# Two transformer blocks on one core: new order and form of the first loads, of one norm, of the weight splits and of two feed-forwards

## The reference

```
layer 0: h += diff_attention(rms(h)); h += (silu(n @ Wg) * (n @ Wu)) @ Wd, n = rms(h)
         h += sigmoid(rms(h) @ Wgate) * (p @ Wp)
layer 1: the same, with neighbourhood attention;  h = rms(h) * norm_final
layer 2: h += even_mixer(rms(h));  h += conv_ffn(rms(h))
layer 3: h += odd_mixer(rms(h));   h += conv_ffn(rms(h));  out = rms(h) * final_norm
rms(x) = x / sqrt(mean(x * x) + 1e-6) * gamma
conv_ffn(n): u, g = n @ W_in;  a = 3-tap causal convolution of u + bias
             return (silu(a) * g) @ W_out                      (hidden width 2816)
```

## Time and profile before

| what | value |
|---|---|
| median of 3 runs | 1296.54 us (1296.34 to 1297.35) |
| the profiled execution, its own time | 1298.22 us |
| its span, first to last instruction | 1296.4 us |
| TensorE busy | 1260.0 us, 97% of the span |
| VectorE busy | 943.4 us, 73% |
| ScalarE busy | 675.2 us, 52% |
| GpSimd busy | 170.3 us, 13% |
| granted TensorE clock, mean | 0.994 of full speed |

### The profile page before, as it was taken

One profiled execution on the slowest core, in us unless ns is written; L12 is line 12 of the kernel. 1 busy time (PEld: TensorE's weight loads), 2 busy tenths in 40 slices (PEclk: granted clock), 3 DMA queues, 4 the chain that ended last, 5 costly groups with the idle time before them and its releaser, 6 DMA issues.

```text
span 1296.4 us, 22210 instructions
## 1 busy us (share of the span) xinstructions
PE 1260.0 (97%) x8648; PEld 1149.5 (89%) x8648; DVE 943.4 (73%) x1208; ACT 675.2 (52%) x971; POOL 170.3 (13%) x168
## 2 busy tenths in 40 slices
PE   6999899999999999999999899999999999999998
PEld 5899788888978888888899899999888889999986
DVE  4798787795777778777557878787757766877743
ACT  5466555544546665555446335555445566554532
POOL 4011211081120010000013702000312001000000
PEclk8999999999999999999999999999999999999999
DMA  7434598756544337775553566975464524766541
GB/s 266 159 128 128 136 246 216 209 170 206 185 150 159 130 99 207 190 194 178 179 197 130 165 207 168 263 197 178 159 203 150 163 100 129 212 185 174 192 163 64
DMA packets 277574, 224.74 MB, mean 173 GB/s; under 512 B 8424, under 2 KB 264432, under 8 KB 277376
## 3 DMA queue, kind: packets, MB, share of 16 engines
q1 hardware_dynamic: 274896, 214.24, 54.6%
q0 software_dynamic: 2608, 9.52, 2.5%
HBM read 222.67 MB, written 2.63 MB: 174 GB/s over the span
## 4 chain that ended last, share of the span: by engine, by line
PE 84%; DVE 9%; ACT 2%; DMA 2%; issue 1%; POOL 1%; SPq 1%; POOLq 0%; ACTq 0%
PE ps L1599 19%; PE ps L1590 13%; PE ps L1591 12%; PE ps L1592 12%; PE ps L1600 10%; DVE wlo L1018 3%; DVE x L1044 3%; PE ps L1598 2%; PE ps L1838 2%; ACT whi L674 2%; PE ps L1803 1%; PE ps L1805 1%; PE ps L1804 1%; PE ps L1862 1%; PE ps L1723 1%; PE ps L1891 1%
## 5 line engine op out<-in xcount | busy, mean ns | idle before, releaser
L1018 DVE TENSOR_TENSOR wlo<-raw,whi 128x2048 fp32r<-128x2048 f32 (+1 forms) x205 | 467.9, 2286 | 134.9 <-ACT whi L674 134.0
L674 ACT CAST whi<-raw 128x2048 fp32r<-128x2048 f32 (+1 forms) x205 | 384.4, 1880 | 232.7 <-PE ps L1592 136.8
L1590 PE MATMUL ps<-x,whi 128*128 128x256 f32 (+1 forms) x1640 | 474.7, 289 | 11.2 <-DVE wlo L1018 5.4
L1591 PE MATMUL ps<-x,whi 128*128 128x256 f32 (+1 forms) x1640 | 464.0, 283 | 0.0
L1592 PE MATMUL ps<-x,wlo 128*128 128x256 f32 (+1 forms) x1640 | 463.9, 283 | 0.0
L1590 PEld LDWEIGHTS ps<-x,whi 128*128 128x128 f32 (+1 forms) x1640 | 313.8, 191 | 21.3 <-issue 9.3
L1591 PEld LDWEIGHTS ps<-x,whi 128*128 128x128 f32 (+1 forms) x1640 | 314.1, 192 | 0.5
L1592 PEld LDWEIGHTS ps<-x,wlo 128*128 128x128 f32 (+1 forms) x1640 | 313.8, 191 | 0.0
L1599 PE MATMUL ps<-x,whi 128*128 128x512 f32 x616 | 222.2, 399 | 2.6 <-DVE wlo L1018 2.6
L1599 PE MATMUL ps<-hid,whi 128*128 128x512 f32 x504 | 177.7, 395 | 1.1 <-DVE hid L1312 1.1
L1600 PE MATMUL ps<-x,wlo 128*128 128x256 f32 x616 | 172.8, 280 | 0.0
(11 more groups left out here) (193 smaller groups left out, 1443.0 us busy)
## 6 DMA issues: line engine op xcount, KB each, us to landing
raw<-in_ffn_w_in SPq DMA_DIRECT2D x88, 512.0 KB, 5.1
raw<-in_ffn_w_gate SPq DMA_DIRECT2D x44, 512.0 KB, 4.0
raw<-in_ffn_w_up SPq DMA_DIRECT2D x44, 512.0 KB, 5.3
raw<-in_ffn_w_out SPq DMA_DIRECT2D x38, 512.0 KB, 4.4
raw<-in_ffn_w_down SPq DMA_DIRECT2D x32, 512.0 KB, 4.4
raw<-in_da_w_qkv SPq DMA_DIRECT2D x24, 512.0 KB, 4.9
raw<-in_na_w_qkv SPq DMA_DIRECT2D x24, 512.0 KB, 4.5
raw<-in_od_w_in SPq DMA_DIRECT2D x24, 512.0 KB, 4.6
```

The costliest lines, as they stand in the source:

```text
L674: nc.scalar.copy(whi[:, c % RING, 0:n], raw[:, c % RING, 0:n]).then_inc(w_hi, 1)
L1018: nc.vector.tensor_tensor(wlo[:, c % RING, 0:n], raw[:, c % RING, 0:n], whi[:, c % RING, 0:n].bitcast(F32), ALU.subtract).then_inc(w_lo, 1)
L1590: mm(dst, hi, x[:, 0, :], start=start, stop=False)
L1591: mm(dst, hi, x[:, 1, :], start=False, stop=False)
```

## The change

Seven edits, listed by their place in time.

1. Start. The gammas and the first x tiles are issued by ScalarE; SP begins with chunk 0 in four pieces of 256 KB, chunk 1 comes in two. The splits of chunks 0 and 1 follow the pieces, and TensorE takes chunk 0 in the order of the pieces. All four squares of the first norm stand ahead of the split of chunk 2. GpSimd makes `gmid` first and issues the constants only when chunk 2 has landed; its additions for the first norm stand behind these issues.
2. `SUM_AT` and `SPREAD_AT` of v0 and v1 move later by half a chunk or less.
3. The double norm: only the plain squares are made (four ScalarE instructions; L724 goes), GpSimd adds nothing, and TensorE forms both sums with 16 small products of the squares by `gsq` (ones and the squared gamma), two columns each.
4. The first product of layer 2 ("ev") gets banks 0, 2, 3, 5 in a written order with `EV_FREE`, and the spread moves from the middle of chunk 2 to the start of chunk 3.
5. `updates`: the low part of one weight chunk is made before the last `lo_x` and not behind it.
6. `ffn2` and `ffn3` use `wide_chunk`; for them ScalarE copies a half bank, VectorE adds and scales.
7. The masks start three chunks later in `down0` and `down2`.

```
-SUM_AT = {"v0": (2, 0), "v1": (2, 0), "v3": (1, 1)}
-SPREAD_AT = {"v0": (3, 0), "v1": (2, 1), "v3": (2, 1)}
+SUM_AT = {"v0": (2, 1), "v1": (2, 1), "v3": (1, 1)}
+SPREAD_AT = {"v0": (3, 1), "v1": (3, 0), "v3": (2, 1)}
-EV_BANKS = (2, 3, 5)
+EV_BANKS = (2, 3, 5, 0, 2, 3, 5, 2)
+EV_FREE = (0, 0, 0, 0, 1, 2, 3, 5)
-FFN_BANKS = (((5, 6), (0, 1), (2, 3)), ((5, 6), (0, 1), (2, 3)), (2, 3, 5), (5, 6, 7))
-DOWN_BANKS = ((0, 2, 5, 0), (0, 2, 5, 0), (0, 6, 0, 6))
+FFN_BANKS = (((5, 6), (0, 1), (2, 3)), ((5, 6), (0, 1), (2, 3)), ((2, 3), (0, 1), (5, 6)),
+             ((5, 6), (0, 1), (2, 3)))
+DOWN_BANKS = ((0, 2, 5, 0), (0, 2, 5, 0), (0, 5, 2, 6))
...
 SP:
-            load_x(0)
-            load_chunk("v0", 0)
+            for a in range(4):
+                cs = slice((a % 2) * 512, (a % 2 + 1) * 512)
+                sp.dma_start(dst[a // 2][:, :, cs], src[a // 2][:, :, cs]).then_inc(w0_in[a], 16)
             load_x(1)
...
 GpSimd:
-            gp.wait_ge(w0_in[1], 16)
+            nc.gpsimd.tensor_tensor(gmid[:], fin, gcol[:, GAM["mix2"]:GAM["mix2"] + KT], ALU.mult)
+            nc.gpsimd.memset(gsq[:, :, 0], 1.0)
+            nc.gpsimd.tensor_tensor(gsq[:, :, 1], fin, fin, ALU.mult).then_inc(gmid_ok, 1)
+            gp.wait_ge(w_in[2], 32)
             gp.dma_start(cst[:], consts[:, 0:NCONST]).then_inc(const_in, 16)
...
-                    gp.wait_ge(w_used, START["down0"])
+                    gp.wait_ge(w_used, START["down0"] + 3)
...
-            gp.wait_ge(w_used, START["down2"])
+            gp.wait_ge(w_used, START["down2"] + 3)
...
 ScalarE:
+            nc.scalar.dma_start(gcol[:], w["gammas"]).then_inc(gcol_in, 16)
+            nc.scalar.dma_start(h[:, 0:2, :], x_source(0)).then_inc(x0_in[0], 16)
...
+            for p in range(4):
+                squares("mix0", p)
             split(2)
-            squares("mix0", 2)
-            squares("mix0", 3)
...
 squares():
+                nc.scalar.activation(to, hpair(p), ACT.Square, scale=D ** -0.5
+                                     ).then_inc(sq_ok, 1)
...
 ScalarE, ffn, conv:
+                        ac.wait_ge(w_used, c0 + 1 + j)
+                        nc.scalar.copy(gu[:, jj, :, :], ps[:, b0:b0 + 2, S:2 * S]
+                                       ).then_inc(part_ok, 1)
                         split(c0 + jj + RING, turn)
...
 VectorE, updates:
+                    if p == 3:
+                        split(last(wname) - 1 + RING)
                     lo_x(name, p)
-                split(last(wname) - 1 + RING)
                 split(last(wname) + RING)
...
 VectorE, ffn, conv:
-                        ve.wait_ge(w_used, c0 + 1 + j)
-                        nc.vector.tensor_tensor(g, b, over2(rst[:]), ALU.mult).then_inc(gu_ok, 1)
+                        ve.wait_ge(part_ok, n)
+                        nc.vector.tensor_tensor(g, ps[:, b0:b0 + 2, 0:S], g, ALU.add
+                                                ).then_inc(sum_ok, 1)
+                        ve.wait_ge(sum_ok, n)
+                        nc.vector.tensor_tensor(g, g, over2(rst[:]), ALU.mult).then_inc(gu_ok, 1)
                         if one:
                             taps(*one)
...
 TensorE, sum_squares:
+                if n == MID:
+                    for k in range(KT):
+                        pe.wait_ge(sq_ok, sq_base(n) + k // 2 + 1)
+                        src = ssum[:, k // 2, :] if k < 4 else sq[:, k // 2 - 2, :]
+                        for t in range(TT):
+                            at = (k % 2) * S + t * P
+                            ins = mm(bank(SS)[:, 2 * t:2 * t + 2], src[:, at:at + P], gsq[:, k, :],
+                                     start=k == 0 and t == 0, stop=k == KT - 1 and t == TT - 1)
...
 TensorE, ffn:
-                    if layer < 2:
-                        wide_chunk(b, c0 + jj, xs[XBUF[name]], KT, name if fresh else None,
-                                   turn, middle=middle)
-                    else:
-                        f_chunk(b, c0 + jj, name, fresh, turn, middle)
+                    wide_chunk(b, c0 + jj, xs[XBUF[name]], KT, name if fresh else None,
+                               turn, middle=middle)
...
 TensorE, ev:
+                if EV_FREE[i]:
+                    pe.wait_ge(copied, COPY_BASE["ev"] + EV_FREE[i])
+                if i == 3:
+                    spread_r("mix2")
+                f_chunk(EV_BANKS[i], START["ev"] + i, "mix2")
```

More of the change, by code:

```diff
@@ L508, in add_squares @@
                 n = NORM[name]
-                per = sums_of(n)
+                total = ssum[:, 0, :]
                 for p in range(1, 4):
[L511 to L521, removed]
-                            gp.wait_ge(add_ok, r)
[L523 to L532, removed]
@@ L707, in squares @@
                 n = NORM[name]
[L708 to L714, removed]
-                    else:
[L716 to L726, removed]
+                r = add_base(n) + p - 1
+                if p == 0 and n:
+                    ac.wait_ge(ss_out, n)
+                if p and n != MID and r >= 2:
+                    ac.wait_ge(add_ok, r - 1)
+                if n == MID:
+                    to = ssum[:, p, :] if p < 2 else sq[:, p - 2, :]
+                else:
+                    to = sq[:, r % 2, :] if p else ssum[:, 0, :]
+                nc.scalar.activation(to, hpair(p), ACT.Square, scale=D ** -0.5
+                                     ).then_inc(sq_ok, 1)
             def pair(name, p):
@@ L912, in _ @@
             take_x("mix0", 0)
-            split_first(0)
-            split_first(1)
+            for q in range(4):
+                split_first(q)
             take_x("mix0", 1)
-            split(1)
+            split_first(4)
+            split_first(5)
             take_x("mix0", 2)
             take_x("mix0", 3)
-            squares("mix0", 0)
-            squares("mix0", 1)
+            for p in range(4):
+                squares("mix0", p)
             split(2)
-            squares("mix0", 2)
-            squares("mix0", 3)
             ac.wait_ge(lam_sum, 2)
@@ L1061, in diagonals @@
                 ve.wait_ge(pow_ok, n + 1)
-                for s in range(sums_of(n)):
+                for s in range(spreads_of(n)):
                     r = tiny[:, 12:14] if s else tiny[:, 6:8]
@@ L1780, in down @@
                         pe.wait_ge(hid_lo, base + 8 * part + D_TILES[part])
-                    if part == 0 and layer < 2 and g < 3:
+                    if part == 0 and g < 3:
                         pe.wait_ge(sum_ok, base + FT - 2 + g)
@@ L2021, in _ @@
             ffn(3)
+            pe.wait_ge(sum_ok, 4 * FT - 1)
             for k in range(KT):
```

149 lines of the change are left out of this document (90 added, 59 removed).

## The result

The changed kernel takes 1299.67 us, the median of 14 runs from 1295.92 to 1302.91. The kernel before, on the same chip, takes 1296.66, the median of 14 runs from 1294.66 to 1297.6. The ratio is 1.0021, with a 95% interval of 1.0011 to 1.003: slower by 0.2%, some 2.7 us, where 4.3 us less was forecast. It lies outside the range, and none of the rivals describes it (D names a time near it, 1299.2, but for a reason that the traces exclude).

What follows compares the result with a forecast made beforehand. TensorE, busy 97% of the span, was taken as the bound, so time could come only from its waits and streaming rate. Terms -5.3 -4.6 +3.3 -4.4 +2.6 +3.2 +2.0 -1.1 gave -4.3: 1292.2 us, range 1285.5 to 1298.5.

Steps and rivals of the forecast that it cites:

- D: Rival: VectorE becomes the bound of the convolution feed-forwards; +2.7 us, 1299.2, at 5.8 us a chunk; chance 0.14.
- part 5: Updates: later x in each first chunk costs +2.6 us of work, and clock falls behind longer waits cost +3.2.
- part 2: Start: earlier squares and sums bring v0's spread to 30 us against 34.99; -4.6 us, bounds -2.5 and -6.5.
- Part 4: Double norm, gates of layer 1 and "ev": faster low parts without GpSimd's additions, earlier pooled product; -4.4 us.
- Part 3: v1: moving the sums later adds a wait for diagonals and delays the gate; +3.3 us, bounds +1.0 and +4.5.
- Part 1: Convolution feed-forwards of layers 2 and 3: 512-column form saves 0.12 us in each of 44 chunks; -5.3 us.
- E: Rival: the 512-column form saves only 2.5 ns per tile product, 3.5 us less; -0.8 us, 1295.7; chance 0.03.
- Part 6: Loads in layer 2: a chunk's load is issued later and TensorE arrives earlier, so it waits; +2.0 us.
- Part 7: Masks and down product: masks moved later remove layer 2's wait for hidden values; -1.1 us.
- Rival B: The clock never falls and the new order in `updates` is free; -10.1 us, 1286.4; chance 0.18.
- C: Rival: GpSimd's constants delay the first sums, start gains only 2.5 us and "ev" 1.5; +0.7, 1297.2; chance 0.17.

Runs made afterwards that it cites:

- the two direct tests: Kernel before with only the new order in `updates`: 1306.0 us, +9.7; changed kernel with only that order undone: 1291.0 us, 7.1 below the changed kernel.
- the old order: Changed kernel with the weight's low part in `updates` put back behind the last pair of x: 1291.0 us, ratio 0.9966 to the kernel before.
- v1's old places: Changed kernel with v1's sums back at (2, 0) and its spread at (2, 1): 1296.25 us, ratio 1.0 to the kernel before.
- the filled one: Changed kernel with 11 to 14 unread matmuls in TensorE's wait for x in each feed-forward's first chunk: 1294.08 us, ratio 0.9991 to the kernel before.
- all three edits: Changed kernel, `updates` order and v1 places undone, chunk 2's high part before the fourth square: 1284.12 us; second version adds six unread matmuls in v1: 1281.7.
- the form alone: Kernel before with only the 512-column form in the feed-forwards of layers 2 and 3: 1292.93 us, ratio 0.9976, -3.1.
- the loads behind the additions: The 1284.12 us version with GpSimd's wait for chunk 2 and four constant loads moved behind its first additions: 1288.11 us, ratio 0.9937 to the kernel before.

## Why the prediction was wrong

Two steps failed: part 5 by 3.4 us, part 2 by 2.4, with 0.8 more just behind it.

**Part 5, the updates, was mis-sized on both terms.** The mechanism was named rightly: a longer wait for x in each first chunk, and a clock that falls behind some. The wait was put at 0.4 us in three layers and 1.4 in the other, 2.6 in all, and measured 0.9 and 1.5, 4.3: I gave the weight's low part 2.2 us, half of a pair made alone, though it moves to where GpSimd is still adding, and there it takes 2.85. The clock was put at two falls by 1.6 us, 3.2; it is 2.5 falls in the mean by some 2 us, 4.9. Together 9.2 for 5.8, with the two direct tests at 9.7 and 7.1. The bounds of this part, 2.6 and 6.4, reach to 9.0, but the range was drawn by the rivals: it had room for this miss alone (-4.3 + 3.4, 1295.6) and not for it and the start together.

**Part 2, the start, failed in its mechanism.** "In the new order the squares are early" holds for three of the four. I followed GpSimd's queue past its loads and not ScalarE's behind it: the ring of two squares makes the fourth wait for GpSimd, and the high part of chunk 2 stood behind that. The copy of `rst` behind the spread is 2.6 us earlier, the lower bound, and 2.2 in the mean of the four profiles with this start (the changed kernel's, the old order's, v1's old places' and the filled one's), for 4.6. With one line of ScalarE's queue changed the spread comes at 29, where the forecast had "30".

A second loss lies at the end of layer 0's attention: at its update the four profiles stand 1.2, 0.7, 0.2 and 3.4 us ahead, 1.4 in the mean. Three of them have a fall of the clock near 130, the fourth has none. This is not shown to come from the start. It follows two waits of TensorE, 0.98 and 1.08 us, that all 13 profiles have alike; the clock fell behind them in six of the eight profiles of the changed kernel and its variants and in none of the five of before and its variants. The first two versions with all three edits run the same instructions up to v1, and it fell in the second alone:

```profile
124.00:128.00 4.00, 2.44 (x18) 2.21 (x19) 1.17 (x4) 2.27 (x2) 0.00 (x0) 1.00 0.69 180
128.00:132.00 4.00, 4.00 (x35) 4.00 (x34) 3.25 (x7) 3.52 (x8) 0.59 (x1) 1.00 0.00 0
```

```profile
124.00:128.00 4.00, 2.51 (x15) 2.27 (x16) 0.83 (x3) 2.27 (x2) 0.00 (x0) 0.86 0.63 168
128.00:132.00 4.00, 4.00 (x27) 4.00 (x27) 2.09 (x4) 2.10 (x5) 0.00 (x0) 0.71 0.00 0
```

Why it never fell there in the kernels made from before stays open. The forecast has no term for it.

**The others.** Part 4 gave -3.1 for -4.4; the low parts of 0.87 and the wait at chunk 5 (1.59, forecast 1.2) were right. The spread came late: at 723.06, less the 2.3 us that the kernel stood behind there, is 720.8 and not 719.9, as the clock fell to 0.57 behind the new narrow sums, which the forecast had at full clock. Part 3 was right within its bounds. Part 1 was right to 0.01 us a chunk in ffn3, though the form alone gives 3.1 us and not 5.3, as the masks take some back in ffn2; with the rate both rivals on it fall: D, as VectorE needs 5.23 us against 5.64, and E by 6.8 ns against 2.5. Part 6 is not there in the changed kernel, 2.0 us in its favour, and one profile in six with the old order and the new form has it, with 1.8; its own terms, 1.45 + 0.7 + 0.2 less a half, make 1.85. Part 7 was larger than said: the masks are worth 0.6 alone and 4.0 beside the new form, since VectorE has less to spare there. Rival B (no falls, order free) asks for what the kernel without the new order has, and that takes 1291.0, 4.6 above B's 1286.4: the start and part 4 gained less. C had the start's small gain and named GpSimd's constants for it, but not how they act, through ScalarE's queue; its 1.5 for "ev" was 3.1. In part 2 the row at 20.88 is one addition and not two; the sum does not rest on it.

Put together: -4.3, +3.2 for the start and the fall near 130, +3.4 for the updates, +1.3 in part 4, -2.0 in part 6 and -0.5 in parts 1 and 7 make +1.1. The median stands at +2.7. Runs of this kernel lie 7 us apart, so the 1.6 between may be falls of the clock; that is argued and not shown, and I can't place it further.

## What to carry to other kernels

When work is put into one queue ahead of other work, walk each engine's queue through the ring buffers it shares with the next one: the cost here was one square waiting for one addition, and what stood behind the square. Price a moved instruction at the place to which it moves, with the neighbours that it has there. Where TensorE is busy 97% of the time, a wait of 2.7 us has two prices, its length and a chance of a slower clock, and a wait of 1.3 us, behind which it never fell here, can be much the cheaper of the two; and when a kernel's runs spread more than they did, compare the mean clock of the runs before believing one trace.

## What the runs showed of the hardware

- The same idle time of TensorE is followed by a fall of the clock in some executions and not in others: 6 of 12 behind 2.67 us, 4 of 4 behind 3.29 us, none of 32 behind the 1.3 us of the old order (eight profiles of four updates each). Idle times of 0.98 and 1.08 us in close order, near 130, were followed by one in 6 of 13.
- The clock also fell with no idle time in front of it, behind the 32 matmuls of two columns that now make the sums in "ev". The changed kernel, TensorE busy throughout:

```profile
712.24 1.85 PE L1596 MATMUL ps<-gsq,ssum 128*128 128x2 f32 x16
```

```profile
712.00:716.00 4.00, 4.00 (x38) 4.00 (x37) 0.46 (x3) 2.75 (x2) 0.00 (x0) 1.00 0.59 195
716.00:720.00 4.00, 4.00 (x23) 4.00 (x23) 2.33 (x3) 0.00 (x0) 3.46 (x5) 0.57 0.28 85
```

  It is there in seven of the eight profiles with these sums, all but that of the loads behind the additions. All five kernels with the old sums have a fall near this place too, but behind waits (0.41, 1.10 and 2.50 us in before). So the narrow matmuls are not shown to be the cause. A row that says busy is no sign that the clock will stay.
- With matmuls that nothing reads in the wait, 11 of 512 columns in 2.7 us or 14 in 3.36, the clock stayed up in four of four updates, where it had fallen in 10 of 16 without them; with six in 1.52 us it stayed up in v1, in one profile.
